# The last expert's gate and up product ahead of the third last expert's down product

## The chip, the cores and the metric

One core of a Trainium2 chip runs the whole layer in one launch. The metric is the device time of one execution in microseconds (us), as the median of some runs; the profile shows one further execution. TensorE does matrix products, VectorE and ScalarE elementwise work, GpSimd indirect transfers, SyncE issues nearly all other DMAs.

## What is computed

A block over 512 tokens of width 1024 in float32: a mixer part (not touched here), then a mixture of experts, then a gated sum and a last norm. From the reference, cut to the parts that matter:

```python
for g in range(N_EXPERT_GROUPS):                 # 4 groups of 8 experts
    hg = silu(einsum('td,edf->tef', t, w_gate[g])) * einsum('td,edf->tef', t, w_up[g])
    hg = hg * combine[:, g, :, None]             # two experts of one group per token
    out = out + einsum('tef,efd->td', hg, w_down[g])
# after it
gate = sigmoid(rmsnorm(h, g_ple) @ ple_gate_w + ple_gate_b)
h = h + gate * (p @ ple_proj_w)
return rmsnorm(h, g_final)
```

Each expert has gate and up weights of 1024x256 and down weights of 256x1024, 1 MB each: 96 MB for the 32 experts.

## The kernel before

**Experts.** The kernel goes through the experts e = 0 to 31, each with at most 64 tokens (a loop for more is there and does not run with these inputs). For each, TensorE does three steps. `gu_step(e)` multiplies the gathered tokens by gate and up weights (32 matmul records of 256 columns), into bank 1 + e % 2. ScalarE's `silu(e)` (line 821) and VectorE's `hidden` (line 922) make the product, in one buffer `vrow`; `h_step(e)` transposes it on TensorE (line 2078) and VectorE copies it out (line 1339). `down_step(e)` multiplies by the down weights (8 matmul records of 512 columns), into bank 4 + e % 2, and ScalarE's `y_out(e)` (line 550) copies the result into one of three buffers. In the loop (line 2119) the order on TensorE is h(e), gate and up of e + 1, down(e), so the elementwise work of an expert lies beside the down product of the one before. At the end that gives: h(29), gate and up of 30, down(29), h(30), gate and up of 31, down(30), h(31), down(31).

**Results.** For e = 0 to 29 GpSimd's `scatter(e)` (line 1579) waits for y_out(e) and writes the rows to `pairs_d` in DRAM, two rows of 1024 for each token. The last two experts are not scattered: their rows are added by `combined(t)` on TensorE, products with a selection matrix, which wait for both copies. After the last scatter is issued GpSimd waits for all of them and sets `moe_done` with a small memset (line 1642).

**Weights.** SyncE loads the 96 pieces in the order of a list `ORDER` of (expert, 0 gate, 1 up, 2 down). Position p of the list has a place in SBUF, `SPOT[p]`, and from 22 on a position `AFTER[p]` whose piece it overwrites; it is issued once that piece's product is done. All go into one DMA queue, each 128 x 8 KB. Both lists are worked out from positions alone.

**End of the stage on SyncE**, in this order: wait for 31 gate and up products, first part of the gate weights of the last stage (1 MB, line 500); wait for `moe_done` and 32 gate and up products, `load_pairs(0)` (1 MB, line 506); wait for 31 down products, second part of the gate weights, `load_h(1)`, `load_pairs(1)`, the other half of the gate weights (2 MB), bias, `load_h(2)`, `load_pairs(2)`, `load_h(3)`; wait for 32 down products, `load_pairs(3)` and the last gains.

**Last stage.** For each of four tiles of 128 tokens VectorE's `combine(t)` waits for the pairs and adds them to h with weights (line 1406, four instructions), then adds the `combined` rows (line 1415, two). TensorE's `turned_h(t)` transposes h (line 2176), VectorE scales it into `ut`, and `gate(n)`, two for each tile, multiplies by the gate weights (line 1653, 16 matmul records each). The order on TensorE is all `combined`, turned_h(0), gate(0), turned_h(1), gate(1), gate(2), turned_h(2) and so on. Sigmoid, sums, norm and store follow.

Of the kernel before, what the change touches and what calls it, by code (L numbers as in the profile page):

```python
# [50 lines left out]
NE = NG * NEG  # L51
# [47 lines left out]
def at(t, parts, off, dims):  # L99

    p0, p1 = parts
    width = t.shape[1]
    return bass.AP(t, p0 * width + off, [[width, p1 - p0]] + [list(d) for d in dims])
# [7 lines left out]
def least(eng, sem, value):  # L111

    if isinstance(value, int) and value <= 0:
        return
    eng.wait_ge(sem, value)
# [18 lines left out]
def build(nc, A, out):  # L134
    ctx = ExitStack()
    with ctx:
# [174 lines left out]
        ROOT4 = tuple(2 * NT + t + 1 for t in range(NT))  # L311


        ORDER = [(0, 0), (0, 1)] + [x for e in range(NE - 1) for x in ((e + 1, 0), (e + 1, 1), (e, 2))] + [(NE - 1, 2)]
        SPOT, AFTER = list(range(NPIECE)), [None] * NPIECE
        for q in range(3 * NE):
            kept = (SPOT[q] in (10, 11) and q >= NPIECE) or (SPOT[q] in (16, 17) and q >= 52)
# [4 lines left out]
        def place(e, k):  # L322

            i = SPOT[ORDER.index((e, k))]
            return ((ring, i * PIECE) if i < 12 else (big, (i - 12) * PIECE) if i < 16 else
                    (zbuf, (i - 16) * PIECE) if i < 18 else (h, (i - 18) * PIECE) if i < 20 else (ut, (i - 20) * PIECE))
# [30 lines left out]
        def most(eng):  # L357

            return eng.value_load(at(flag, (0, 1), 0, [[1, 1]]), min_val=0, max_val=T)
# [7 lines left out]
        def weights(eng, p):  # L367

            e, k = ORDER[p]
            if e < 2 and k < 2:  # L370
# [7 lines left out]
        def _(sp):  # L378
# [96 lines left out]
            for p in range(NPIECE, 3 * NE):  # L475
                e, k = ORDER[AFTER[p]]
                if AFTER[p] == 34:
# [69 lines left out]
        def _(act):  # L547
# [270 lines left out]
            def silu(e):  # L818
                act.wait_ge(gu_ps, e + 1)
                least(act, hg_sb, 2 * e)  # L820
                act.activation(at(moe, (0, CAP), M_SG, [[1, DE]]), at(bank[1 + e % 2], (0, CAP), 0, [[1, DE]]),  # L821
                               ACT.Silu).then_inc(sg_sb, 1)

            def y_out(e):
                act.wait_ge(dn_ps, e + 1)
                least(act, ys_stored[e % YBUF], stores(e))
                copy(at(moe, ALL, M_Y + e % YBUF * 512, [[1, 512]]), bank[4 + e % 2][:, :], dn_sb)

            def slots_30_out():

                act.wait_ge(ppt_ps, 2)
                copy(at(small, ALL, S_S30, [[1, 2 * P]]), bank[1][:, 0:2 * P], ppt_sb)
                copy(at(rw, ALL, 0, [[1, 2 * P]]), bank[1][:, 2 * P:4 * P], ppt_sb)

            def p_rows_out():
                act.wait_ge(ppt_ps, 3)
                for j in range(2):
                    copy(at(ring, ALL, E_PPT + j * T, [[1, T]]), bank[PP_BANK[j]][:, :], ppt_sb)
                copy(at(ring, ALL, E_S, [[1, T]]), bank[7][:, :], ppt_sb)

            def pp_out(n):
                act.wait_ge(pp_ps, n + 1)
                copy(at(zbuf, ALL, n * 512, [[1, 512]]), bank[PP_BANK[n % 2]][:, :], pp_done)

            silu(0)
            for e in range(NE):
                if e + 1 < NE:
                    silu(e + 1)
                if e == P_ROWS:
                    p_rows_out()  # L850
                if e in P_PROJ:
                    for n in range(2):
                        pp_out(2 * P_PROJ.index(e) + n)
                if e == 0:
                    slots_30_out()
                    act.wait_ge(slot_done, 1)
                y_out(e)
# [793 lines left out]
        def _(pe):  # L1651
# [368 lines left out]
            def p_rows():  # L2020

                pe.wait_ge(ld_ppw, 32)
                pe.wait_ge(xT_sb, P_ROWS + 3)
                for k in range(NT):
                    for j in range(2):
                        rows = pe.transpose(bank[PP_BANK[j]][:, k * P:(k + 1) * P], rv(E_PIN + k * DPLE + j * P, P), ident)
                rows.then_inc(ppt_ps, 1)

            def proj(e, n):
                t, half = n // 2, n % 2  # L2030
                pe.wait_ge(ppt_sb, 4)
                pe.wait_ge(xT_sb, e + 3)
                for j in range(2):
                    got = mm(bank[PP_BANK[n % 2]][:, :], rv(E_PPT + j * T + t * P, P),
                             rv(E_PPW + j * DM + half * 512, 512), j == 0, j == 1)
                got.then_inc(pp_ps, 1)
# [27 lines left out]
            def gate_up(k, odd, gate_w, up_w, dst, rows=0, between=None):  # L2064

                for j in range(KC):
                    if rows and j % 4 == 0:
                        pe.wait_ge(xT_sb, rows - 1 + j // 4)
                    if between and j == 4:
                        between()  # L2070
                    for n, w in enumerate((gate_w, up_w)):
                        last = mm(bank[dst][n * CAP:(n + 1) * CAP, 0:DE],
                                  at(moe, ALL, M_XT + k * DM + j * P + odd * CAP, [[1, CAP]]),
                                  at(w[0], ALL, w[1] + j * DE, [[1, DE]]), j == 0, j == KC - 1)
                return last

            def h_rows():
                return pe.transpose(bank[3][:, 0:P], vrow[:, :], ident)  # L2078

            def down(k, w, dst):  # L2080

                for j in range(2):
                    for n in range(2):
                        last = mm(bank[dst][n * CAP:(n + 1) * CAP, :], at(moe, ALL, M_HT + k * P + j * CAP, [[1, CAP]]),
                                  at(w[0], ALL, w[1] + j * DM + n * 512, [[1, 512]]), j == 0, j == 1)
                return last

            def x_step(q):
                pe.wait_ge(xg_ready[q % XBUF], (q + 1) // XBUF * 16)
                least(pe, xT_sb, 2 * q)  # L2090
                x_rows(q % XBUF)

            def gu_step(e, between=None):
                pe.wait_ge(gu_ready[e % LOADS], (e // LOADS + 1) * 32)
                least(pe, hg_sb, 2 * (e - 1))
                gate_up(e // 2 % 2, e % 2, place(e, 0), place(e, 1), 1 + e % 2, e // 2 * 2 + 2,
                        between).then_inc(gu_ps, 1)

            def h_step(e):
                pe.wait_ge(hg_sb, 2 * e + 2)  # L2100
                least(pe, hT_sb, e)
                h_rows().then_inc(hT_ps, 1)

            def down_step(e):
                pe.wait_ge(hT_sb, e + 1)
                pe.wait_ge(down_ready[e % LOADS], (e // LOADS + 1) * 16)
                least(pe, dn_sb, e - 1)
                down(e % 2, place(e, 2), 4 + e % 2).then_inc(dn_ps, 1)
# [7 lines left out]
            h_step(1)  # L2116
            x_step(1)
            pe.wait_ge(ppt_sb, 2)
            for e in range(1, NE):
                if e > 1:  # L2120
                    h_step(e)
                if e % 2 == 0 and e + 2 < NE:
                    if e == P_ROWS + 1:
                        pe.wait_ge(ppt_sb, 4)
                    if e - 1 in P_PROJ:
                        pe.wait_ge(pp_done, 2 * P_PROJ.index(e - 1) + 2)
                    x_step(e // 2 + 1)
                if e + 1 < NE:
                    gu_step(e + 1)
                if e == P_ROWS:  # L2130
                    p_rows()
                if e in P_PROJ:
                    for n in range(2):
                        proj(e, 2 * P_PROJ.index(e) + n)
                down_step(e)
            pe.wait_ge(slot_done, 1)
            with pe.If(most(pe) > CAP):
                with pe.Fori(1, ROUNDS) as r:
# [74 lines left out]
```

## Time and profile before

| | us |
|---|---|
| median of 3 runs | 512.49 |
| lowest and highest | 511.51, 515.82 |
| span of the profiled execution | 512.3 |
| TensorE busy in it | 477.8 (93%) |
| VectorE, ScalarE, GpSimd busy | 232.3, 169.8, 149.9 |

The profiled execution stands close to the median. The page shows the DMA engines busy in nine tenths or more of nearly every slice from about 220 to 420 us, at some 420 GB/s. The chain that ended last is the work followed back from the last instruction, each step to what released it. In a timeline, PE is TensorE, PEld its weight loads, DVE VectorE, ACT ScalarE, POOL GpSimd, SPq the DMA issues of SyncE; "idle before" is the time that the engine stood still ahead of the row and what ended it. The granted clock (PEclk) is a share of 2.4 GHz.

### The profile page before, as it was taken

How to read it: one execution, taken by the hardware profiler on the slowest of the kernel's cores; microseconds unless marked ns; L12 is line 12 of the kernel's file. 1: busy time of each engine (PE TensorE's matmuls, PEld its weight loads, DVE VectorE, ACT ScalarE, POOL GpSimd, SP SyncE). 2: the span in 40 equal slices, each digit the busy share in tenths (PEclk: the TensorE clock that was granted, in tenths of full speed). 3: DMA queues.
4: the chain of work that ended last, by engine and by line, in shares of the span. 5: the costliest groups of instructions: out<-in, count | busy, mean ns of one | idle time of the engine just before them, and what ended most of it. 6: DMA issues, size and time to landing. Idle time of an engine off the chain costs nothing.

```text
span 512.3 us, 7264 instructions
## 1 busy us (share of the span) xinstructions
PE 477.8 (93%) x2718; PEld 264.5 (52%) x2718; DVE 232.3 (45%) x683; ACT 169.8 (33%) x283; POOL 149.9 (29%) x136
## 2 busy tenths in 40 slices
PE   3799999999999999989999999987999997999993
PEld 3355555744854457655555555543454553444441
DVE  2899948999233258642222222220211211565525
ACT  6633576547442333111111111120122111214454
POOL 1079999614100001222222222220121210003250
PEclk9999999999999999999999999997999998999998
DMA  8874300399499986899999999999999996990022
GB/s 299 145 202 93 70 0 2 125 155 168 156 357 412 421 339 221 316 391 421 419 418 419 418 414 417 419 418 420 420 421 419 416 406 228 399 371 2 0 82 82
DMA packets 60140, 144.73 MB, mean 283 GB/s; under 512 B 27587, under 2 KB 36839, under 8 KB 47817
## 3 DMA queue, kind: packets, MB, share of 16 engines
q1 hardware_dynamic: 54504, 133.92, 71.0%
q0 software_dynamic: 5328, 10.31, 5.3%
q8 instruction: 22, 0.36, 0.3%
q14 instruction: 14, 0.11, 0.1%
q10 hardware_dynamic: 272, 0.04, 0.0%
HBM read 138.17 MB, written 14.19 MB: 297 GB/s over the span
## 4 chain that ended last, share of the span: by engine, by line
PE 69%; DMA 18%; SPq 5%; DVE 3%; issue 2%; ACT 2%; POOL 0%; DVEq 0%; POOLq 0%
PE bank L1653 63%; DMA ring<-in_exp_w_up_dram 6%; DMA big<-in_exp_w_up_dram 6%; DMA moe<-v_d,gidx_all 4%; SPq L388 3%; DMA pairs_d<-moe,sidx_all 2%; PE bank L2059 1%; PE bank L1753 1%; SPq L364 1%; PE bank L1743 1%; PE bank L2078 1%; PE bank L1916 1%; PE bank L2176 1%; DVE moe L922 1%; SPq L393 1%
## 5 line engine op out<-in xcount | busy, mean ns | idle before, releaser
L1653 PE MATMUL bank<-ring,moe 128*64 128x256 f32 (+2 forms) x848 | 112.0, 410 | 3.7 <-DMA ring<-in_exp_w_up_dram 3.2
L1653 PEld LDWEIGHTS bank<-ring,moe 128*64 128x64 f32 x848 | 60.8, 140 | 40.7 <-issue 15.6
L1579 POOL DMA_INDIRECT pairs_d<-moe,sidx_all x32 | 31.8, 993 | 155.0 <-PE bank L2059 78.9
L922 DVE TENSOR_TENSOR vrow<-moe,bank 64x128 f32<-64x128 f32 x64 | 18.7, 291 | 118.3 <-ACT moe L821 117.3
L1653 PE MATMUL bank<-ut,big 128*128 128x512 f32 x128 | 57.7, 597 | 1.2 <-ACT ut L562 1.2
L821 ACT ACTIVATE moe<-bank 64x256 f32<-64x256 f32 x32 | 12.1, 377 | 138.2 <-PE bank L1653 138.2
L550 ACT ACTIVATE moe<-bank 128x512 f32<-128x512 f32 (+1 forms) x65 | 36.5, 582 | 60.6 <-PE bank L1653 50.5
L1653 PE MATMUL bank<-ring,ut 128*128 128x512 f32 x128 | 55.7, 593 | 0.4 <-DVE ut L922 0.4
L1653 PE MATMUL bank<-big,moe 128*64 128x256 f32 (+1 forms) x264 | 43.2, 440 | 3.0 <-DMA big<-in_exp_w_up_dram 2.6
L922 DVE TENSOR_TENSOR ring<-ring,bank 128x64 f32<-128x64 f32 (+1 forms) x142 | 39.5, 278 | 2.8
L1653 PEld LDWEIGHTS bank<-ring,ut 128*128 128x128 f32 x128 | 24.0, 190 | 29.3 <-issue 29.3
L1653 PEld LDWEIGHTS bank<-ut,big 128*128 128x128 f32 x128 | 23.4, 190 | 27.7 <-issue 25.3
L922 DVE TENSOR_TENSOR bank<-bank,ring 128x64 f32<-128x64 f32 (+1 forms) x142 | 35.2, 287 | 3.3 <-PE bank L1753 0.5
L1653 PE MATMUL bank<-ring 128*64 128x128 f32 (+1 forms) x128 | 32.5, 437 | 0.0
L1653 PEld LDWEIGHTS bank<-big,moe 128*64 128x64 f32 x264 | 21.9, 142 | 15.8 <-issue 5.3
L1339 DVE COPY moe<-bank 128x128 f32<-128x128 f32 x32 | 9.3, 292 | 45.1 <-PE bank L2078 45.1
L922 DVE TENSOR_TENSOR moe<-bank,vec 128x512 f32<-128x512 f32 x40 | 26.0, 686 | 7.5 <-PE bank L2059 5.6
L1653 PE MATMUL bank<-big,ut 128*128 128x512 f32 x64 | 28.3, 595 | 0.0
L1653 PE MATMUL bank<-big,zbuf 128*128 128x512 f32 x64 | 28.2, 594 | 0.0
L550 ACT ACTIVATE zbuf<-bank 128x512 f32<-128x512 f32 x18 | 12.6, 704 | 33.9 <-PE bank L1653 33.8
L1653 PEld LDWEIGHTS bank<-ring 128*64 128x64 f32 (+1 forms) x128 | 15.2, 163 | 15.3 <-issue 15.0
L1653 PE MATMUL bank<-h,moe 128*64 128x256 f32 (+1 forms) x96 | 22.1, 454 | 0.0
(198 smaller groups left out, 616.8 us busy)
## 6 DMA issues: line engine op xcount, KB each, us to landing
ring<-in_exp_w_gate_dram SPq DMA_DIRECT2D x19, 1024.0 KB, 23.8
ring<-in_exp_w_down_dram SPq DMA_DIRECT2D x18, 1024.0 KB, 26.9
ring<-in_exp_w_up_dram SPq DMA_DIRECT2D x17, 1024.0 KB, 20.2
big<-in_exp_w_up_dram SPq DMA_DIRECT2D x7, 1024.0 KB, 20.1
big<-in_exp_w_down_dram SPq DMA_DIRECT2D x7, 1024.0 KB, 18.2
big<-in_exp_w_gate_dram SPq DMA_DIRECT2D x6, 1024.0 KB, 20.6
ut<-in_exp_w_up_dram SPq DMA_DIRECT2D x4, 1024.0 KB, 24.0
h<-in_exp_w_down_dram SPq DMA_DIRECT2D x4, 1024.0 KB, 23.0
```

The costliest lines, as they stand in the source:

```text
L364: eng.dma_start(at(to[0], ALL, to[1], [[1, PIECE]]), w[e].rearrange("(p j) f -> p (j f)", p=P)).then_inc(done, 16)
L388: sp.dma_start(at(ring, (d * NS, d * NS + NS), R_BRAW + n * G * CH, [[CH, G], [1, CH]]), dr(A[name], d * G * NS * CH, [[CH, NS], [NS * CH, ...
L393: sp.dma_start(at(ring, ALL, R_CRAW + n * 4 * P + d * NS, [[P, NB], [1, NS]]), dr(A[name], d * G * CH * NS, [[NS, P], [GB * CH * NS, NB], ...
L550: act.activation(o, i, ACT.Copy).then_inc(signal, 1)
L821: act.activation(at(moe, (0, CAP), M_SG, [[1, DE]]), at(bank[1 + e % 2], (0, CAP), 0, [[1, DE]]), ACT.Silu).then_inc(sg_sb, 1)
L922: return dve.tensor_tensor(o, a, b, op)
L1339: dve.tensor_copy(at(moe, ALL, M_HT + (e % 2) * P, [[1, P]]), bank[3][:, 0:P]).then_inc(hT_sb, 1)
L1579: pool.indirect_dma_start(pairs, bass.IndirectOffsetOnAxis(ap=index, axis=0), at(moe, ALL, M_Y + k * 512, [[1, 512]]), None, bounds_check= ...
L1653: return pe.matmul(o, a, b, start=start, stop=stop, skip_group_check=loose)
L1743: last = pe.transpose(bank[E_BANK[b] + ri][:, q * P:(q + 1) * P], es_rows(b, q // 2, (q % 2 * 2 + ri) * P, P), ident)
L1753: last = pe.transpose(bank[B_WT + ri][:, (g % 4) * P:(g % 4 + 1) * P], rv(R_W + ri * 1024 + g * P, P), ident)
L1916: rows = pe.transpose(bank[H_BANK[t] + n][:, (j % 4) * P:(j % 4 + 1) * P], at(h, ALL, t * DM + j * P, [[1, P]]), ident)
```

## The change

The order of the last steps on TensorE becomes: h(29), gate and up of 30, gate and up of 31, h(30), down(29), h(31), down(30), down(31). The order of the last pieces in `ORDER` follows: positions 91, 92, 93 hold gate 31, up 31, down 29 instead of down 29, gate 31, up 31; 94 and 95, down 30 and down 31, are as before. ScalarE does silu(30), silu(31), y_out(29), y_out(30), y_out(31) instead of alternating. VectorE, GpSimd and the waits of SyncE are not edited.

```diff
-        ORDER = [(0, 0), (0, 1)] + [x for e in range(NE - 1) for x in ((e + 1, 0), (e + 1, 1), (e, 2))] + [(NE - 1, 2)]
+        ORDER = [(0, 0), (0, 1)] + [x for e in range(NE - 3) for x in ((e + 1, 0), (e + 1, 1), (e, 2))]
+        ORDER += [(NE - 2, 0), (NE - 2, 1), (NE - 1, 0), (NE - 1, 1), (NE - 3, 2), (NE - 2, 2), (NE - 1, 2)]
@@ ScalarE
             for e in range(NE):
-                if e + 1 < NE:
+                if e + 1 < NE - 1:
                     silu(e + 1)
+                if e == NE - 3:
+                    silu(NE - 1)
@@ TensorE
-            for e in range(1, NE):
+            for e in range(1, NE - 3):
                 if e > 1:
                     h_step(e)
...
-                if e + 1 < NE:
-                    gu_step(e + 1)
+                gu_step(e + 1)
...
                 down_step(e)
+            h_step(NE - 3)
+            gu_step(NE - 2)
+            gu_step(NE - 1)
+            h_step(NE - 2)
+            down_step(NE - 3)
+            h_step(NE - 1)
+            down_step(NE - 2)
+            down_step(NE - 1)
```

## Rows read from the trace of the kernel before

**Rows 1.** Chain that ended last, in order of time: start us, us, what

```profile
391.90 2.13 SPq L364
...
396.25 31.17 DMA big<-in_exp_w_up_dram
...
434.97 1.96 PE bank L1653 x8
...
437.70 7.21 PE bank L1653 x32
...
446.37 7.10 PE bank L1653 x16
...
483.57 20.61 PE bank L1653 x48
```

**Rows 2.** Timeline, 418 to 450: start us, us, engine, line, operation, idle before

```profile
419.21 5.39 PE L1653 MATMUL bank<-ring,moe 128*64 128x256 f32 x40
...
422.92 0.38 SPq L500 DMA_DIRECT2D ring<-in_ple_gate_w_dram  x1
422.93 0.38 ACT L821 ACTIVATE moe<-bank 64x256 f32<-64x256 f32 x1 [3.27 <-PE bank L1653]
...
424.65 0.60 ACT L550 ACTIVATE moe<-bank 128x512 f32<-128x512 f32 x1 [1.34 <-PE bank L1653]
...
426.02 0.98 POOL L1579 DMA_INDIRECT pairs_d<-moe,sidx_all  x1 [4.60 <-ACT moe L550]
...
427.46 6.86 PE L1653 MATMUL bank<-big,moe 128*64 128x256 f32 x40 [2.60 <-DMA big<-in_exp_w_up_dram]
...
432.66 0.38 ACT L821 ACTIVATE moe<-bank 64x256 f32<-64x256 f32 x1 [7.41 <-PE bank L1653]
...
433.40 0.09 POOL L1642 MEMSET fill<- 1x1 int32 x1 [6.41 <-issue]
...
438.96 2.99 DVE L1406 SCALAR_TENSOR_TENSOR h<-big,small,h 128x512 f32<-128x512 f32 x4 [4.04 <-DMA big<-pairs_d]
...
442.05 1.41 DVE L1415 SCALAR_TENSOR_TENSOR h<-h,small,bank 128x512 f32<-128x512 f32 x2
...
444.84 1.09 PE L2176 MATMUL bank<-cst,h 128*128 128x128 f32 x8
...
446.93 2.99 DVE L1406 SCALAR_TENSOR_TENSOR h<-big,small,h 128x512 f32<-128x512 f32 x4
```

**Rows 3.** DMA issues (count, KB each, us to landing) at 391.9, 426, 422.9, 433.5, 136.6, 509.2, all

```profile
ring<-in_exp_w_down_dram SPq DMA_DIRECT2D x1, 1024.0 KB, 29.9
...
pairs_d<-moe,sidx_all POOLq DMA_INDIRECT x1, 6.3
...
ring<-in_ple_gate_w_dram SPq DMA_DIRECT2D x1, 1024.0 KB, 13.5
...
big<-pairs_d SPq DMA_DIRECT2D x1, 1024.0 KB, 5.4
...
ring<-in_glu_w_dram SPq DMA_DIRECT2D x1, 1024.0 KB, 5.3
...
out_dram<-ring SPq DMA_DIRECT2D x2, 256.0 KB, 2.0
...
pairs_d<-moe,sidx_all POOLq DMA_INDIRECT x32, 6.9
```

**Rows 4.** Windows: stretch; busy PE, PEld, DVE, ACT, POOL; PEclk, DMA share, GB/s

```profile
221.50:223.10 1.60, 0.01 (x1) 0.01 (x1) 0.74 (x5) 1.13 (x3) 0.53 (x1) 1.00 1.00 397
349.90:352.00 2.10, 0.00 (x0) 0.00 (x0) 0.27 (x1) 0.33 (x1) 0.99 (x1) 0.99 1.04 421
352.00:358.40 6.40, 5.33 (x26) 3.05 (x28) 0.00 (x0) 0.00 (x0) 0.01 (x1) 0.50 1.01 422
...
427.00:430.20 3.20, 2.74 (x14) 1.60 (x16) 0.00 (x0) 0.00 (x0) 0.00 (x0) 0.51 0.65 258
430.20:434.00 3.80, 3.80 (x30) 1.80 (x26) 0.58 (x2) 0.38 (x1) 0.09 (x1) 0.96 0.25 99
```

## The prediction

> **What bounds the kernel now.** I read the chain that ended last first, in order of time. Before 396 us it alternates between TensorE and the issue of weight loads. Then it follows one load, the last expert's up weights, for 31 us until 427.42, and after that it is TensorE with short steps of other engines until 504.18 [rows 1]. So the stretch I care about has two bounds: up to 427 the weight stream, which TensorE has caught up with; after 446.37 an unbroken run of gate products on TensorE. Whatever moves the start of the first gate product moves the end by the same amount: 512.3 - 446.37 = 65.9 us follow it.
>
> Second I read the timeline from 419 to 446 [rows 2], because two paths meet at the first gate product:
>
> - TensorE's own: gate and up of expert 31 and the down product of 30 from 427.46, the down product of 31, end at 434.97 + 1.96 = 436.93, the combine products 437.70 to 444.91, then the transposes of h at 444.84 [rows 1, 2].
> - The way of the results: expert 29 is the last whose rows are scattered. ScalarE copies its down product at 424.65, GpSimd scatters at 426.02 and sees the scatter landed at 433.40, SyncE then loads the first pairs, VectorE starts on them at 438.96 (it had waited 4.04 us for them) and adds them up until 443.46 [rows 2]. The copy to VectorE's start is 14.3 us: 1.37 to the scatter, 7.38 to its landing, 5.56 to the pairs.
>
> How far is the second from deciding? The transposes need the first half of h, ready at 442.05 + 0.71 = 442.76 (half of the two sums' 1.41), some 442.8 with the semaphore; TensorE came at 444.84. So that path has 2.0 us of slack. From VectorE's start to the gate product it would take 3.84 us to the transposes and 446.37 - 444.84 = 1.53 to the gate: 5.4 us.
>
> **What the change removes: one place of waiting in the weight stream.** The up weights of 31 go from place 93 to 92, the gate weights from 92 to 91, the down weights of 29 from 91 to 93. The release rules go by place, and neither the tile nor the release of a place changes, so the places are issued at the same times. How much earlier does place 92 land than 93? Place 91 landed at 391.90 + 29.9 = 421.8 and place 93 at 396.25 + 31.17 = 427.4 [rows 1, 3]: two loads in 5.6 us, 2.8 for one. (I do not use the landing time shown for a gate load, as it shares its semaphore with the up load.) Place 92 lands at 424.6; gate and up of 31 start at 424.7, 2.8 us earlier. The down weights of 29 now land at 427.4, before they are wanted.
>
> **Does TensorE stay at full clock?** Gate and up of 30 end at 422.9, where their SiLU starts. h of 30 is now queued behind gate and up of 31, so TensorE idles 1.8 us until 424.7. An idle stretch of 1.6 us left the granted clock at 1.00, stretches of 3.2 us (2.10 and 6.40 - 5.33 = 1.07) and of 2.6 us (ahead of 427.46) were followed by 0.50 and 0.51 [rows 2, 4]. 1.8 is nearer to the first, so I take full clock: 3.72 us from start to the SiLU, as at 419.21 to 422.93. At the lower of the clock's two levels, 1.2 instead of 2.4 GHz, the same product took 5.20 us (427.46 to 432.66), so the wrong answer costs 1.5 us [rows 2].
>
> **What it moves: the down product of 29.** After gate and up of 31 (SiLU at 424.7 + 3.7 = 428.4) come h of 30, 0.28 us, and the down product, 1.72 us by 422.93 to 424.65. The copy for 29 starts at 430.4 instead of 424.65: 5.75 us later [rows 2]. ScalarE has its SiLU of 31 ahead of that copy, but is idle by then. Behind it stand, as before, the scatter, GpSimd's wait for all scatters, and on SyncE everything queued behind that wait: first pairs, second part of the gate weights, h, second pairs, the rest. All are issued later by the same amount, and VectorE's sums wait for them.
>
> **TensorE's own path.** After the down product of 29: h of 31, 0.28, whose product on VectorE has had the 2.0 us of h and down of 29; down of 30, 1.7; down of 31 without the gap that it had ahead of 434.97, 1.96. End: 430.4 + 0.3 + 1.7 + 2.0 = 434.4, combine products until 434.4 + 0.77 + 7.2 = 442.4. That is a gain of 2.5 us [rows 1], of which nothing arrives if the other path is later. The down weights of 31 keep their place; should they come up to 1 us late, it lies under the same cover. If the other path were free, 2.5 us would be gained.
>
> **Sum of the other path.** Copy 430.4; plus 14.3 gives 444.7 for VectorE's start if each step costs what it did. What may get cheaper is the landing of the scatter, 6.3 us from its issue [rows 3]. That was measured from 426 on, while the stream was full, and at 430.2 to 434 the DMA share was still 0.25 [rows 4]: a minority of the engines was behind with loads, and the first gate weights, issued 422.92, landed only at 422.92 + 13.5 = 436.4 [rows 2, 3]. The scatter now goes out at 431.8. Bounds: below, the 2.0 us of a 256 KB store in the quiet end of the kernel; above, the median 6.9 us of all scatters [rows 3]. It still meets the laggards until 436.4, so I take 5.0, nearer to the upper row: 1.3 saved. The pairs landed 5.4 us after their issue, behind those gate weights; a 1 MB load into a quiet queue took 5.3 [rows 3], so nothing is saved there. VectorE starts at 443.4 and the gate product at 443.4 + 5.4 = 448.8: 2.4 us later than 446.37.
>
> The Trainium skill, in "DMA: Bandwidth & Descriptors", section "Anatomy of one DMA — SWDGE (gpsimd) path", prices a DMA of this kind at 2.0 us plus its bytes over 436 GB/s; for 256 KB that is an estimate of 2.6 us. The scatters of this case took 6.3 to 6.9, so the trace does not bear it out while loads run; by that price the gate product would start at 446.4, no later than before.
>
> **The restart of the clock.** TensorE now idles from 442.4 to 447.2 (443.4 + 3.84), 4.8 us, longer than both stretches after which the clock was 0.50. After the first of these, 5.3 us of work ran at the lower level, a loss of 2.7; after the second, 1.5 was lost [rows 1, 2, 4]. Below, nothing is lost if the idling is short. Some of the slow time will lie in the waits for VectorE between the transposes and the gate product, so I take 1.2.
>
> The later gate products hold: VectorE came to the second pairs at 446.93, 8.0 us after the first, and did not wait for them [rows 2]. It needs 4.4 more, so h is ready 12.4 after its start at the latest, and TensorE wants it at 5.4 + 7.1 + restart, 12.5 or more. If the transfers fall further behind, what is missing there comes on top.
>
> **Sum.** 2.4 + 1.2 = 3.6 us later: span 512.3 + 3.6 = 515.9. The median of the runs is 512.49, 0.2 from that span, so 516.0.
>
> **The rivals.**
>
> - Slower by over 1% because gate and up of 31 restart at the lower clock. With rows at 1.6 and 2.6 us of idling I let it decide from their middle, 2.1, that is if they start after 425.0: place 92 landing 0.3 us later than worked out. Then 0.3 + 1.5 us go onto the path: 3.6 + 1.8 = 5.4, about 518. For it: loads are not evenly 2.8 us apart. Against: 2.8 is itself the slower spacing.
> - The scatter lands quickly, and the path of the pairs is no bound. It decides if the scatter lands in under 2.6 us: 6.3 - 2.0 = 4.3 saved against the 1.3 taken, hence 2.4 - 3.0 = -0.6, and an idling of under 2 us, no restart: 511.7. For it is the quiet store of 2.0 us, against it the laggards. (This is the case by the skill's price.)
> - The change does not bring the up weights forward, because what lags is not the place but the transfer. Gate and up start at 427.46 at half clock, copy at 427.46 + 5.2 + 2.0 = 434.7, 10.0 later; the queue is quiet then and the scatter 2.5 us quicker; 444.4 + 10.0 - 2.5 = 451.9, 5.5 later, plus 1.5 for the restart: 519.5. Against it are the even spacings of the landings.
>
> **Chances.** Forecast case 0.57 (its own range 513.5 to 517.6, from scatter landings of 3.5 to 6.3 us), restart at 31 0.23, quick scatter 0.12, no earlier landing 0.08. This kernel can tell about 1% from no change, here 5.1 us. Slower by over 1%: the second and fourth nearly whole, with a few hundredths of the first for a long restart, 0.33. Faster by over 1% needs 5.1 us, twice what TensorE's path gains: 0.02. The rest, 0.65, is within. The range 512.3 to 520.0 leaves out most of the quick scatter and, above, all price bounds together (0.6 + 1.3 + 1.5 + 1.5 over the forecast, 521).
>
> **What would show it.** Gate and up of 31 at 424.7 (not 427.4) at granted clock 1.00; the copy for 29 at 430.4; GpSimd's memset at 437.9; VectorE waiting for pairs until 443.4; TensorE idle some 5 us between combine and transposes, with 0.50 after it; first gate product at 449 to 450; from there 65.9 us. I am wrong if TensorE goes from the combine products to the transposes without a gap, if the up weights land at 427, or if gate products further on wait for pairs or weights.

## Result and profile after

| | before | changed |
|---|---|---|
| median us (6 runs each, in the same sessions) | 514.33 | 518.12 |
| lowest and highest | 511.51, 515.82 | 517.70, 519.74 |
| ratio, 95% interval | | 1.0081 (1.0054 to 1.0107) |
| span of the profiled execution | 512.3 | 516.1 |

The changed kernel is 3.8 us slower by the medians and by the two spans, 4.2 us by the ratio; 3.6 had been forecast. That is within the 1% that counted as no change, though the upper end of the interval touches it. A run's time is some 1.9 us above its span in every run listed with both (518.04 and 516.1 for the profiled run of the changed kernel), so times are compared with times here and spans with spans. The median of before had been 512.49 in the first three runs; over six it is 1.8 higher.

The chain that ended last of the changed kernel, in order of time (start us, us, what). It answers to [rows 1]:

```profile
393.92 30.52 DMA big<-in_exp_w_up_dram
...
424.48 3.67 PE bank L1656 x32
428.15 0.26 PE bank L2081
428.41 1.89 PE bank L1656 x8
430.33 0.61 ACT moe L551
...
431.70 4.59 DMA pairs_d<-moe,sidx_all
...
437.52 4.68 DMA big<-pairs_d
...
446.12 1.97 PE bank L2186 x8
448.11 9.23 PE bank L1656 x16
457.34 0.88 PE bank L2186 x8
```

Before, the chain stayed on TensorE from 427.46 on. Now it leaves TensorE at 430.33 with the copy of expert 29 and comes back at 446.12: copy, scatter, pairs, VectorE's sums. The copy is 430.33 - 424.65 = 5.7 us late. From the copy to the signal for the pairs it took 1.7 us less than before, from the signal to VectorE's start 0.7 less, and 2.1 of slack (442.76 to 444.84) were there: 1.3 us are left. The same stretch in the timeline answers to [rows 2]:

```profile
423.12 0.38 ACT L822 ACTIVATE moe<-bank 64x256 f32<-64x256 f32 x1 [4.76 <-PE bank L1656]
...
428.20 0.38 ACT L822 ACTIVATE moe<-bank 64x256 f32<-64x256 f32 x1 [4.70 <-PE bank L1656]
...
434.93 1.14 PE L1656 MATMUL bank<-moe,small 64*128 64x512 f32 x4 [0.78 <-ACT moe L551]
...
437.41 0.09 POOL L1645 MEMSET fill<- 1x1 int32 x1 [4.73 <-issue]
...
441.01 1.13 PE L1656 MATMUL bank<-moe,ring 64*128 64x512 f32 x4
442.23 2.99 DVE L1409 SCALAR_TENSOR_TENSOR h<-big,small,h 128x512 f32<-128x512 f32 x4 [11.36 <-DMA big<-pairs_d]
...
446.12 1.97 PE L2186 MATMUL bank<-cst,h 128*128 128x128 f32 x8 [3.98 <-DVE h L1418]
```

TensorE's own path did get shorter: the combine products start at 434.93 instead of 437.70, 2.8 us earlier. Then it stands still for 4.0 us, waiting for VectorE. The windows show the granted clock before, in and after this gap (busy PE, PEld, DVE, ACT, POOL; PEclk, DMA share, GB/s):

```profile
424.50:428.20 3.70, 3.70 (x33) 2.31 (x33) 0.00 (x0) 0.00 (x0) 0.00 (x0) 1.00 0.93 356
...
436.00:438.00 2.00, 2.00 (x12) 1.17 (x10) 0.00 (x0) 0.59 (x2) 0.09 (x1) 1.00 0.00 0
...
442.10:444.00 1.90, 0.04 (x1) 0.00 (x0) 1.74 (x3) 0.00 (x0) 0.00 (x0) 1.00 1.05 407
446.00:448.10 2.10, 1.97 (x8) 1.59 (x9) 1.42 (x3) 1.31 (x3) 0.00 (x0) 0.50 0.98 407
448.10:452.00 3.90, 3.89 (x5) 1.82 (x6) 3.68 (x6) 0.13 (x1) 0.00 (x0) 0.50 1.05 388
452.00:454.00 2.00, 2.00 (x5) 0.76 (x4) 1.41 (x2) 0.55 (x1) 0.00 (x0) 0.90 1.05 392
```

Gate and up of 31 ran at 1.00. The transposes and most of the first gate product ran at 0.50, the lower of the two levels: 1.97 us instead of 1.09, and 9.23 instead of 7.10.

So the 3.8 us are two terms. The transposes start 446.12 - 444.84 = 1.3 us later. From there to the end of the first gate product it took 457.34 - 446.12 = 11.2 us instead of 453.47 - 444.84 = 8.6, which is 2.6 us for the restart. Everything after it kept its duration.

### The profile page after: what moved, and what is told of

It reads as the page before. It is cut to its first block, busy times and chain, and to the rows that moved or that the text cites. A ratio compares the mean times of both kernels' runs of the same rounds, so it can differ in the third digit from the quotient of the medians.

```text
span 516.1 us, 7264 instructions
## 1 busy us (share of the span) xinstructions
PE 477.6 (93%) x2718; PEld 263.6 (51%) x2718; DVE 232.3 (45%) x683; ACT 169.8 (33%) x283; POOL 150.2 (29%) x136
## 4 chain that ended last, share of the span: by engine, by line
PE 66%; DMA 20%; SPq 5%; issue 4%; DVE 3%; ACT 2%; POOL 0%; POOLq 0%; DVEq 0%
PE bank L1656 59%; DMA ring<-in_exp_w_up_dram 6%; DMA big<-in_exp_w_up_dram 6%; DMA moe<-v_d,gidx_all 6%; SPq L389 3%; PE bank L2062 2%; PE bank L1756 1%; DMA big<-pairs_d 1%; DMA pairs_d<-moe,sidx_all 1%; PE bank L2186 1%; PE bank L1746 1%; SPq L365 1%; PE bank L1919 1%; PE bank L2081 1%; ACT moe L551 1%
## 5 line engine op out<-in xcount | busy, mean ns | idle before, releaser
L1656 PEld LDWEIGHTS bank<-ring,moe 128*64 128x64 f32 x856 | 61.9, 139 | 43.7 <-issue 13.8
L1656 PE MATMUL bank<-ring,ut 128*128 128x512 f32 x128 | 57.8, 611 | 0.0
```

What stands on the lines that cost most here:

```text
L1656: return pe.matmul(o, a, b, start=start, stop=stop, skip_group_check=loose)
```

## The experiments

My theory: the move delays the copy of 29 by 5.7 us and with it the signal that releases the pairs. Quicker transfers give some of this back, and the rest uses up 2.0 us of slack; what remains reaches the gate products, and the idle stretch that it opens on TensorE is paid a second time as a restart at the lower clock. Rivals: the cost comes from the new place of the loads; or from transfers behind the pairs; or the slow first gate product waits for operands and not for the clock.

Ratios are of times, against the kernel before in the same sessions, with the 95% interval. Spans are of one profiled execution, 512.3 for the kernel before; in the sessions of the experiments its executions had spans from 509.7 to 514.3, so a difference of two single spans is the weaker evidence of the two.

### The last scatter left out

Both kernels, with expert 29's rows left at zero, so that this part of the result is missing:

```diff
-            for x in (NE - 2, NE - 1):
+            for x in (NE - 3, NE - 2, NE - 1):
                 rows_out(2, sidx_all[:, x:x + 1], ys_stored[2])
-            for e in range(NE - 2):
+            for e in range(NE - 3):
```

Kernel before:

> The kernel before, without the scatter of expert 29's rows at its end: its rows in DRAM stay zero (written early), so part of the result is left out, and GpSimd has only the scatter of 28 to wait for. My account: the way of the results has 2.0 us of slack in the kernel before, so taking its last scatter away gains nothing: within 0.5 us, first gate product still some 8.7 us after the last expert's gate and up product ends. If the scatter were already the bound before the change (no slack), up to 5 us are gained.

Measured: ratio 1.0007 (0.9990 to 1.0024), span 511.7. The signal came at 426.83 instead of 433.40, and nothing was gained.

```profile
432.09 0.38 ACT L821 ACTIVATE moe<-bank 64x256 f32<-64x256 f32 x1 [7.27 <-PE bank L1653]
432.13 0.33 SPq L506 DMA_DIRECT2D big<-pairs_d  x1
```

This agrees with a results' way that was no bound, but it is a weaker test than it looks. The load of the pairs also waits for the 32nd gate and up product, and so left at 432.13, only 1.4 us earlier than at 433.52. Without slack about that much would have been gained, not the 5 us of the expectation; the interval allows a gain of 0.5 us at most. (Its 8.7 us are wrong too: the first gate product started 13.7 us after the last gate and up product ended, in this run as in the kernel before.) The stronger evidence on the slack is the late signal below.

Changed kernel:

> The changed kernel with the same scatter left out (expert 29's rows stay zero). My account: TensorE's own path is left, which ends its combine products at 442.1; the transposes follow without a gap, the first gate product starts near 443.6 at granted clock 1.00, and the span is some 2.5 to 3 us below the kernel before (509.5 to 510), 6.5 below the changed kernel. Rival, that the loss comes from transfers behind the pairs (gate weights, second pairs) or from the new place of the loads and not from the scatter: the span stays at 514 to 516.

Measured: ratio 0.9962 (0.9946 to 0.9979), span 509.7. Timeline of that run:

```profile
427.95 0.33 SPq L507 DMA_DIRECT2D big<-pairs_d  x1
...
442.28 1.31 PE L2186 MATMUL bank<-cst,h 128*128 128x128 f32 x8 [0.25 <-DVE h L1418]
...
443.81 7.10 PE L1656 MATMUL bank<-ring,ut 128*128 128x512 f32 x16 [0.22 <-DVE ut L925]
```

The pairs leave at 427.95, the transposes follow the combine products almost at once, and the gate product starts at 443.81 and takes 7.10. With the same loads and the same order on TensorE, leaving out the wait for one scatter takes 6.4 us off the span. Without it the loads and TensorE's order gain 2.6 us by the spans (512.3 to 509.7) and 2.0 by the ratio, where the sum had TensorE's path at 2.5. Even here the 0.25 us ahead of the transposes are a wait for VectorE: the pairs, issued while loads were still landing, took 10.4 us, and the two paths meet almost exactly. The rival that blames the loads falls. This run alone does not settle the rival of later transfers, since everything queued behind the pairs left earlier with them. The trace of the changed kernel does: its chain goes from the first pairs to the transposes, and from the end of the first gate product to the end of the run it took 58.8 us, as before, so nothing further on waited longer.

### A late signal in the kernel before

Nothing but memsets on GpSimd between the landing of the last scatter and the signal:

```diff
+            pool.wait_ge(xT_ps, NE)
+            for _ in range(6):                 # 2 in the other run
+                seq(pool.memset(at(moe, ALL, M_XG, [[1, DM]]), 0.0))
```

Six:

> The same with six memsets, 6.2 us. The pairs then go into an emptied queue (4.7 us instead of 5.4). My account: 6.2 - 0.7 - 2.0 = 3.5 us later, and TensorE, idle by then for 3.5 us, restarts at the lower clock, 2.6 us more: 6 us slower, span 518.4, though TensorE's order is that of the kernel before. Rival, that the loss in the changed kernel comes from the order on TensorE and not from the late signal: below 2 us.

Measured: ratio 1.0114 (1.0080 to 1.0148), that is 5.9 us, span 518.2.

```profile
432.45 6.00 POOL L1611 MEMSET moe<- 128x1024 f32 x6 [5.48 <-DMA pairs_d<-moe,sidx_all]
...
444.49 2.99 DVE L1406 SCALAR_TENSOR_TENSOR h<-big,small,h 128x512 f32<-128x512 f32 x4 [9.63 <-DMA big<-pairs_d]
...
448.38 1.97 PE L2180 MATMUL bank<-cst,h 128*128 128x128 f32 x8 [3.53 <-DVE h L1415]
...
450.38 9.06 PE L1657 MATMUL bank<-ring,ut 128*128 128x512 f32 x16
```

With TensorE's old order and the old loads a late signal alone makes the whole picture of the changed kernel: a gap of 3.5 us before the transposes, 1.97 for them, 9.06 for the first gate product. The transposes are 448.38 - 444.84 = 3.5 us late. From their start to the end of the first gate product it took 11.06 us instead of 8.63, so the restart adds 2.4.

Two:

> The kernel before, with two memsets of 1 us on GpSimd (2.1 us) between the landing of the last scatter and the signal for the pairs. My account by a slack of 2.0 us: 0 to 0.3 us slower. If the way of the results has no slack: 2 us slower.

Measured: ratio 1.0026 (1.0007 to 1.0044), 1.3 us, where at most 0.3 had been expected; the span was 511.9, below that of before. The trace shows why both can be:

```profile
427.39 5.39 PE L1657 MATMUL bank<-big,moe 128*64 128x256 f32 x40 [2.41 <-DMA big<-in_exp_w_up_dram]
...
432.71 1.96 POOL L1611 MEMSET moe<- 128x1024 f32 x2 [5.60 <-DMA pairs_d<-moe,sidx_all]
...
444.53 1.31 PE L2180 MATMUL bank<-cst,h 128*128 128x128 f32 x8 [1.17 <-DVE h L1415]
```

In this execution the gap of 2.41 us ahead of gate and up of 31 did not lower the clock, so TensorE's path was 1.5 us shorter. The results' way was ready at 444.53, 1.7 later than the 442.8 worked out for before, and was the bound. Where that product runs at the lower clock, as in the trace of before, 444.53 still lies ahead of TensorE's 444.84 and costs nothing. Where it runs at full clock, TensorE is ready at 443.38 (the last run below), and the delay costs 1.2 us.

That does not explain the 1.3 us of the ratio. A mix of such executions costs between nothing and 1.2, and 1.2 only if all of them run that product at full clock. The last run below makes that product run at full clock and gains 1.8 us, which speaks for the lower clock in most executions of the kernel before. The interval here reaches down to 0.4 us, so the slack is not refuted, but this test leaves its size open below 2 us.

### One half of the change at a time

Only the loads:

```diff
+        ORDER += [(NE - 2, 0), (NE - 2, 1), (NE - 1, 0), (NE - 1, 1), (NE - 3, 2), (NE - 2, 2), (NE - 1, 2)]
```

(with the rest of the `ORDER` edit, and no edit on TensorE and ScalarE)

> Only the loads of the change: the order of TensorE as before, down weights of 29 two places later. The down product of 29 then waits for them until 427.4 (4.5 us idle) and starts at half clock, gate and up of 31 follow it. My account: copy of 29 near 430.9, VectorE's sums of the first pairs near 443, transposes near 447, little or no idling before them, so no restart: 2 to 3 us slower than before. Rival, that the load order itself is harmless: no change.

Measured: ratio 1.0052 (1.0034 to 1.0070), 2.7 us, span 514.0. The down product of 29 waits until 426.92, its copy starts at 429.74, and the transposes at 446.53 without a gap before them; the first gate product took 7.10. The size was as expected, but not quite the place: TensorE's own path ended last. VectorE's sums were done at 446.42, and the first half, which is all that the transposes need, some 0.7 us before that.

Only the order on TensorE and ScalarE, with `ORDER` as before:

> Only the order of TensorE and ScalarE of the change, with the loads as before. Gate and up of 31 wait until 427.4 after 4.5 us idle and run at half clock (5.2 us), the copy of 29 comes near 434.7, 4.4 later than in the changed kernel. My account: VectorE starts on the first pairs near 446.3, the restart is paid after it: 4 us slower than the changed kernel, 8 slower than before, span near 520. Rival, that the place of the loads gained nothing in the change: equal to the changed kernel, 516.

Measured: ratio 1.0155 (1.0119 to 1.0191), 8.0 us, span 519.8.

```profile
428.14 5.36 PE L1655 MATMUL bank<-big,moe 128*64 128x256 f32 x32 [4.34 <-DMA big<-in_exp_w_up_dram]
...
450.65 1.32 PE L2185 MATMUL bank<-cst,h 128*128 128x128 f32 x8 [3.18 <-DVE h L1417]
```

Without the earlier place of the up weights gate and up start at 428.14 after 4.34 us idle, at half clock, and take 5.36 us instead of 3.67; the copy of 29 follows at 435.68. The transposes then ran at 1.00 after 3.18 us idle, and the clock fell only in the first gate product, which took 8.80 us. The new place of the loads is thus worth 519.8 - 516.1 = 3.7 us to the changed order, and each half alone is slower than before.

### The clock by itself

Products of no use keep TensorE busy in the changed kernel's gap, ahead of the last tile's combine products:

```diff
+            def busy(n, dst):
+                for _ in range(n):
+                    mm(bank[dst][:, :], ident, at(cst, ALL, 0, [[1, 512]]), True, True)
...
             for t in range(NT):
+                if t == NT - 1:
+                    busy(8, 6)                 # 4 in the second run
                 combined(t)
```

With 8:

> The changed kernel with 8 products of no use (identity by constants, 0.43 us each, 3.4 us) on TensorE ahead of the last tile's combine products, inside its gap of 4.0 us; all of the result is computed. My account: the granted clock stays at 1.00, transposes to gate product take 1.5 us again instead of 2.0 and the first gate product 7.1 instead of 9.2: 2.6 us less than the changed kernel, span 513.5, still 1.3 over the kernel before. Rival, that the slow first gate product waits for operands or weights: no change, 516.

Measured: ratio 1.0095 (1.0062 to 1.0128), span 516.3. My price of one such product was wrong by a factor of two: they took

```profile
439.91 7.13 PE L1656 MATMUL bank<-cst 128*128 128x512 f32 x16
```

and not 3.4 us. (I had taken the 0.43 us of a matmul record for a product; each product is two records, 0.89 us.) They pushed the transposes to 448.90. The clock did stay at 1.00 and the first gate product took 7.10, so this run separated the two terms, but the net gain did not show. With 4:

> The changed kernel with 4 products of no use on TensorE ahead of the last tile's combine products. One such product takes 0.89 us and not 0.43 (16 records took 7.13 us in the run with 8), so 4 fill 3.5 us of the gap of 4.0 us. My account: granted clock 1.00 throughout, transposes when VectorE is done (446.1 on the changed kernel's clock), gate product 1.5 us after them, taking 7.1 us: span 2.6 us below the changed kernel, 513.5, some 1.3 over the kernel before. Rival, that the restart costs nothing net: 516.

Measured: ratio 1.0028 (1.0015 to 1.0041), span 514.1, 2.0 us below the changed kernel; by the ratios it is 2.7.

```profile
440.78 3.70 PE L1656 MATMUL bank<-cst 128*128 128x512 f32 x8
...
446.64 1.31 PE L2193 MATMUL bank<-cst,h 128*128 128x128 f32 x8 [0.24 <-DVE h L1418]
...
448.18 7.10 PE L1656 MATMUL bank<-ring,ut 128*128 128x512 f32 x16 [0.22 <-DVE ut L925]
```

VectorE started on the pairs 0.5 us later in this execution (442.75 for 442.23), and the gate product took 7.10 us again. From the transposes to the end of that product it took 1.54 + 7.10 = 8.64 us against 11.22 in the changed kernel: 2.6 us for the restart. What remains over the kernel before, 1.4 us by the ratio, is the late transposes (446.64 for 444.84 in this execution). The rival of slow operands falls.

### The same in the kernel before

There the gap of 2.6 us lies ahead of gate and up of 31:

```diff
+                if e + 1 == NE - 1:
+                    pe.wait_ge(hg_sb, 2 * e)
+                    busy(5, 2)                 # 2 in the second run
```

With 5:

> The kernel before with 5 such products (2.2 us) in the gap of 2.6 us ahead of the last expert's gate and up product. My account: that product starts at 427.5 as before but at full clock and ends 1.5 us earlier; the way of the results has 2.0 us of slack, of which 0.5 is left, so the whole 1.5 us arrive: 0.3% faster, span 510.8. If the slack is less than I think, the gain is less; if the clock at that place does not matter, none.

Measured: ratio 1.0010 (0.9996 to 1.0025), span 512.4. The same wrong price: 4.46 us of filling in a gap of 2.6 delayed gate and up to 429.11, which cost what the clock gave. With 2:

> The kernel before with 2 such products (1.8 us) in the gap of 2.6 us ahead of the last expert's gate and up product, which then starts at 427.4 as before, at full clock, and takes 3.7 instead of 5.2 us. My account: TensorE's own path 1.5 us shorter, slack of the results' way 2.0: span 510.8, 0.3% faster. If the way of the results has less slack than 1.5 us, the gain is cut to that slack.

Measured: ratio 0.9965 (0.9951 to 0.9978), 1.8 us faster, span 510.8 as expected.

```profile
425.09 1.88 PE L1653 MATMUL bank<-cst 128*128 128x512 f32 x4
...
427.48 5.39 PE L1653 MATMUL bank<-big,moe 128*64 128x256 f32 x40 [0.51 <-DMA big<-in_exp_w_up_dram]
...
443.38 1.09 PE L2184 MATMUL bank<-cst,h 128*128 128x128 f32 x8
```

The 32 + 8 records take 5.39 instead of 6.86 us and the transposes start 1.5 us earlier. This version computes all of the result and beats both kernels, by a small amount that is clear of the noise.

## Why the prediction was right

- **Bound and slack.** Two paths meeting at the first gate product, with the results' way 2.0 us short of deciding: shown by the late signal (six memsets put VectorE's start at 444.49, 5.5 us late, and the transposes only 3.5 us late) and by the changed kernel itself (1.3 us late at the transposes). The first 2 us of delay were not free in the timed runs, as above, and that stays open.
- **Earlier weights.** Place 92 was worked out to land at 424.6; it landed at 424.44, and gate and up started at 424.48, where 424.7 had been forecast.
- **Clock at gate and up of 31.** Full clock, as taken. The idle stretch was 1.4 us: the trace shows another wait of 1.42 us ahead of gate and up of 30, since this execution came there about 1.3 us earlier; that moved nothing, as the loads were the bound.
- **Copy of 29.** Forecast 430.4, measured 430.33.
- **Scatter and pairs.** The scatter was put at 5.0 us and landed in 4.6; the pairs were put at 5.4, nothing saved, and took 4.7. Together with the 0.1 of the copy and the signal, VectorE started at 442.23, 1.2 earlier than forecast. The step that the pairs save nothing was the wrong one: in the kernel before they had queued behind the first gate weights, in the new one the queue was empty (DMA share 0.00 in 436 to 438). The 5.3 us of the load of glu_w, which I took for a quiet queue, was no measure of it; why that load took longer is not shown.
- **Later transposes.** 1.3 us late, where 2.4 had been worked out. The first gate product came at 448.11, not at 449 to 450, and TensorE's gap was 4.0 us, not some 5.
- **Restart.** This term was mis-sized: 1.2 taken, 2.6 measured, near the 2.7 that stood as the upper bound. I had thought that part of it would lie in waits for VectorE; the transposes, the gap to the gate product and the gate product itself all lay on the path (0.5 and 2.1).
- The two errors, 1.1 too much and 1.4 too little, cancel in the sum. It came out at 515.9 against a span of 516.1, better than its terms, and that closeness is luck.
- **From span to median.** The median was put at 516.0, 0.2 over the span; it was 518.12. The 0.2 compared a span with the time of other runs, and a run's time is 1.9 over its own span. The difference between the kernels does not suffer from this. In the last rival the sum is 519.3, not 519.5 (512.3 + 5.5 + 1.5).
- **Own path of TensorE.** 442.4 forecast for its end, 442.1 measured, and 2.6 us gained by the spans in the run without the scatter.
- **The Trainium skill's price** for a DMA of this kind ("DMA: Bandwidth & Descriptors", "Anatomy of one DMA — SWDGE (gpsimd) path"), an estimate of 2.6 us for 256 KB, is below the landings read here: 6.3 with the queues full, 4.6 with them nearly empty, 3.8 in the run where the order alone was changed and the scatter went out at 437.05. So the case that hung on it did not come.

## What to carry to other kernels

An operation that is moved back takes everything with it that its result releases; follow it to the signal and to what is queued behind that signal before counting what the move gains on the busy engine. When two paths meet, the one with a little slack decides as soon as the slack is used up. The idle stretch that then opens on TensorE was paid again here at the lower clock, 2.6 us for a gap of 4.0. If a gap is unavoidable, a few products of no use inside it can be worth it, as in two runs here, but their length must be measured and be shorter than the gap: in the two runs where it was longer nothing was gained.

## What was not expected of the hardware

- The length of a gap does not by itself say whether the clock falls. Gaps of 2.41 us (the run with two memsets) and 2.24 us (the kernel before without the scatter) stand at the same place, ahead of gate and up of 31. Windows from 427.0 and 426.6 on, of the one and of the other:

```profile
427.00:430.20 3.20, 2.81 (x26) 1.92 (x28) 0.00 (x0) 0.00 (x0) 0.11 (x1) 1.00 0.59 236
```

```profile
426.60:430.00 3.40, 3.31 (x16) 1.98 (x18) 0.00 (x0) 0.00 (x0) 0.09 (x1) 0.52 0.58 230
```

  The longer gap kept 1.00, the shorter was followed by 0.52. The same holds of the stretch of 3.2 us in front of 353 that the prediction read as followed by the lower clock [rows 4]. In the run with two memsets it was as long, and the product behind it took 3.67 us, full clock; in the changed kernel it was shorter, and the product took 5.36:

```profile
353.05 3.67 PE L1657 MATMUL bank<-ring,moe 128*64 128x256 f32 x32 [3.27 <-DMA ring<-in_exp_w_up_dram]
```

```profile
352.78 5.36 PE L1656 MATMUL bank<-ring,moe 128*64 128x256 f32 x32 [3.06 <-DMA ring<-in_exp_w_up_dram]
```

  So neither the line at 2.1 us of idling nor the row at 3.2 can carry a forecast. This may be part of why the kernel before spreads over 4 us between runs; that was only argued.
- Between the landing of the last scatter (431.70 + 4.59 = 436.3) and the signal for the pairs (437.41) GpSimd needs 1.1 us for its own waits and branches. It lies on the chain. The rows of before held it too: landing at 426.02 + 6.3 = 432.3, signal at 433.40 [rows 2, 3].
- The restart cost 2.6 us after a gap of 4.0, 2.4 after one of 3.5, and 1.5 after one of 2.6, each measured on the products that followed. That looks like a rule, but it is none: it cost 1.7 us after 4.34 and after 3.18 us (the run with the old loads) and 1.7 after 2.24 (7.08 us for the 40 records that take 5.39 at full clock, in the kernel before without the scatter).
